# Loading and splitting x and the first two weight slabs in small pieces, in the order of the k tiles

## The reference, cut to what matters

```python
def _rmsnorm(x, g):
    xf = x.astype(jnp.float32)
    y = xf * lax.rsqrt(jnp.mean(xf * xf, axis=-1, keepdims=True) + EPS)
    return (y * g.astype(jnp.float32)).astype(x.dtype)
...
    for l in range(DEPTH):
        h = _rmsnorm(x, g_mix[l])
        p = h @ w_in[l]
```

## Time and profile before

| | |
|---|---|
| runs | 1286.05, 1285.48, 1284.99 us, median 1285.48 |
| profiled execution | span 1283.8 us from the first to the last instruction; no other time of its own is given |
| mean granted TensorE clock | 0.958 |
| busy, share of the span | PE 92%, DVE 58%, ACT 38%, POOL 36% |
| DMA | 108.65 MB, mean 85 GB/s |

### The profile page before, as it was taken

One profiled execution on the slowest core, in us unless ns is written; L12 is line 12 of the kernel. 1 busy time (PEld: TensorE's weight loads), 2 busy tenths in 40 slices (PEclk: granted clock), 3 DMA queues, 4 the chain that ended last, 5 costly groups with the idle time before them and its releaser, 6 DMA issues.

```text
span 1283.8 us, 16689 instructions
## 1 busy us (share of the span) xinstructions
PE 1184.6 (92%) x5302; PEld 963.6 (75%) x5302; DVE 740.4 (58%) x812; ACT 490.1 (38%) x649; POOL 462.8 (36%) x199
## 2 busy tenths in 40 slices
PE   7999999998699979998899999999979999699967
PEld 6788878777588757886778888777757887588856
DVE  5335476677616773377633356757772377716764
ACT  5644244443314432233456323344332343313341
POOL 3423124333443334433533322333333433353341
PEclk8999999999799989998899999999989999899979
DMA  6222113222222222222422211222223222232211
GB/s 256 83 82 72 45 50 99 81 68 81 93 94 75 82 82 89 91 82 82 139 95 68 83 66 36 83 79 69 81 80 99 89 75 82 82 98 84 81 66 66
DMA packets 31681, 108.65 MB, mean 85 GB/s; under 512 B 3722, under 2 KB 3850, under 8 KB 31628
## 3 DMA queue, kind: packets, MB, share of 16 engines
q1 hardware_dynamic: 30396, 105.85, 24.8%
q10 hardware_dynamic: 1232, 2.12, 0.5%
HBM read 105.85 MB, written 2.10 MB: 84 GB/s over the span
## 4 chain that ended last, share of the span: by engine, by line
PE 46%; DVE 36%; ACT 8%; issue 6%; DVEq 2%; ACTq 1%; DMA 1%
DVE arena L830 25%; PE acc L877 10%; PE acc L879 10%; PE acc L878 10%; ACT arena L503 6%; DVE arena L823 5%; PE acc L993 2%; PE acc L994 2%; PE acc L995 2%; DVE arena L835 1%; PE side L1044 1%; DVE xg_lo L554 1%; ACT feat_hi L514 1%; PE side L1064 1%; DVE ssq L561 1%
## 5 line engine op out<-in xcount | busy, mean ns | idle before, releaser
L267 POOL TENSOR_TENSOR w_lo<-w_raw,w_hi 128x1024 fp32r<-128x1024 f32 x192 | 462.2, 2411 | 793.8 <-ACT w_hi L276 793.8
L830 DVE SCALAR_TENSOR_TENSOR arena<-arena,conv_sb 128x512 f32<-128x512 f32 x176 | 322.7, 1833 | 112.3 <-ACT arena L503 99.5
L877 PE MATMUL acc<-xg_hi,w_hi 128*128 128x512 f32 x864 | 345.0, 399 | 15.0 <-POOL w_lo L267 13.7
L879 PE MATMUL acc<-xg_hi,w_lo 128*128 128x512 f32 x864 | 339.1, 392 | 0.0
L878 PE MATMUL acc<-xg_lo,w_hi 128*128 128x512 f32 x864 | 338.9, 392 | 0.0
L276 ACT ACTIVATE w_hi<-w_raw 128x1024 fp32r<-128x1024 f32 x192 | 201.4, 1053 | 251.9 <-PE acc L879 207.1
L877 PE MATMUL acc<-feat_hi,w_hi 128*128 128x512 f32 x480 | 199.8, 416 | 66.4 <-POOL w_lo L267 42.8
L877 PEld LDWEIGHTS acc<-xg_hi,w_hi 128*128 128x128 f32 x864 | 163.5, 189 | 57.6 <-issue 20.9
L878 PE MATMUL acc<-feat_lo,w_hi 128*128 128x512 f32 x480 | 197.0, 410 | 0.0
L879 PE MATMUL acc<-feat_hi,w_lo 128*128 128x512 f32 x480 | 196.1, 408 | 0.0
L879 PEld LDWEIGHTS acc<-xg_hi,w_lo 128*128 128x128 f32 x864 | 163.4, 189 | 34.5
(11 more groups left out here) (133 smaller groups left out, 940.0 us busy)
## 6 DMA issues: line engine op xcount, KB each, us to landing
w_raw<-slabs SPq DMA_DIRECT2D x192, 512.0 KB, 3.3
x<-xT ACTq DMA_DIRECT2D x4, 512.0 KB, 9.6
outT<-arena SPq DMA_DIRECT2D x8, 256.0 KB, 2.1
ln_sb<-ln_gb SPq DMA_DIRECT2D x2, 512.0 KB
spatial_sb<-spatial_w SPq DMA_DIRECT2D x2, 256.0 KB
spatial_b_sb<-spatial_b SPq DMA_DIRECT2D x2, 256.0 KB
gate_sb<-gate_w SPq DMA_DIRECT2D x2, 130.0 KB
rank_raw<-rank_w SPq DMA_DIRECT2D x1, 256.0 KB, 10.5
```

Source lines behind the costliest of these rows:

```text
L267: pool.tensor_tensor(w_lo[:, w], w_raw[:, w], w_hi[:, w].bitcast(F32), ALU.subtract).then_inc(lo_done, 1)
L830: dve.scalar_tensor_tensor(out=z[j], in0=y[j][:, tap:tap + S], scalar=conv_sb[:, bass.ds(coef + tap, 1)], in1=z[j], op0=ALU.mult, op1=ALU. ...
L877: pe.matmul(out, wh, ah, start=first, stop=False)
L879: return pe.matmul(out, wl, ah, start=False, stop=last)
```

## The change

x is loaded in six groups of tiles (0), (1), (2), (3), (4, 5), (6, 7), in turn by ACT's queue (groups 0, 2, 4) and by SP's (1, 3, 5). Slabs 0 and 1 are loaded in three parts each, the columns of k tiles 0 and 1 (128 KB), 2 and 3 (128 KB), 4 to 7 (256 KB), split by ACT and by POOL in the same parts. Semaphores for the parts are added. SP issues rank_raw and slabs 2 and 3 behind these; the other loads keep their order. In the second layer loading and splitting is by whole slabs, as before, but TensorE's order of products is the new one in both layers, with conditions on L for the waits. On DVE gain_lo of 4 and 5 stands ahead of the first two add_square, and add_square of 2 to 5 ahead of rank_lo. ACT's squares are placed between its gains and splits.

The diff, cut to its core:

```diff
--- before.py
+++ after.py
@@ -55,6 +55,9 @@
...
+
+X_GROUPS = ((0,), (1,), (2,), (3,), (4, 5), (6, 7))
+W_PARTS = (slice(0, 2 * P), slice(2 * P, 4 * P), slice(4 * P, SLAB))
 
 def encoder(nc, xT, slabs, rank_w, gate_w, spatial_w, spatial_b, ln_gb, gains, gla_gain, conv, consts, outT):
@@ -164,7 +167,10 @@
             return slot(12 + m)
 
-        x_loaded = [sem(f"x_loaded{i}") for i in range(4)]
+        x_loaded = [sem(f"x_loaded{i}") for i in range(len(X_GROUPS))]
+        raw_part = [[sem(f"raw_part{j}_{part}") for part in range(2)] for j in range(2)]
+        hi_part = [sem(f"hi_part{j}") for j in range(2)]
+        lo_part = [sem(f"lo_part{j}") for j in range(2)]
         gains_loaded, par_loaded = sem("gains_loaded"), sem("par_loaded")
         rank_loaded, vec_loaded = sem("rank_loaded"), sem("vec_loaded")
         raw_loaded = [sem(f"raw_loaded{i}") for i in range(RING)]
@@ -216,6 +222,12 @@
 
             eng.sem_inc(waits_passed, 1)
 
+        def load_x(eng, g):
+            first, n = X_GROUPS[g][0], len(X_GROUPS[g])
+            rows = xT[first * P:(first + n) * P, :].rearrange("(k p) s -> p k s", p=P)
+            eng.dma_start(x[:, first * S:(first + n) * S].rearrange("p (k s) -> p k s", k=n),
+                          rows).then_inc(x_loaded[g], 16)
+
         block = ctx.enter_context(nc.Block())
 
@@ -228,11 +240,29 @@
                              slabs[bass.ds(L * NS + q * RING + j, 1), :, :].rearrange("o p n -> (o p) n")
                              ).then_inc(raw_loaded[j], 16)
 
+            def load_part(j, part):
+                w = W_PARTS[part]
+                sp.dma_start(w_raw[:, j * SLAB + w.start:j * SLAB + w.stop],
+                             slabs[j:j + 1, :, w].rearrange("o p n -> (o p) n")
+                             ).then_inc(raw_part[j][part] if part < 2 else raw_loaded[j], 16)
+
+            load_part(0, 0)
+            load_part(1, 0)
+            load_x(sp, 1)
+            load_part(0, 1)
+            load_part(1, 1)
+            load_x(sp, 3)
+            load_part(0, 2)
+            load_part(1, 2)
+            load_x(sp, 5)
+            sp.dma_start(rank_raw[:, 0:DEPTH * RW], rank_w).then_inc(rank_loaded, 16)
+            load_slab(0, 0, 2)
+            load_slab(0, 0, 3)
             with sp.Fori(0, DEPTH) as L:
-                for j in range(RING):
-                    load_slab(L, 0, j)
+                with sp.If(L > 0):
+                    for j in range(RING):
+                        load_slab(L, 0, j)
                 with sp.If(L < 1):
-                    sp.dma_start(rank_raw[:, 0:DEPTH * RW], rank_w).then_inc(rank_loaded, 16)
                     sp.dma_start(consts_sb[:, :], consts).then_inc(vec_loaded, 16)
                     sp.dma_start(gla_sb[:, :], gla_gain).then_inc(vec_loaded, 16)
                     sp.dma_start(conv_sb[:, :], conv).then_inc(vec_loaded, 16)
@@ -260,7 +290,20 @@
             pool.memset(ones, 1.0).then_inc(ones_set, 1)
             pool.memset(rank_split[:, 2 * RW:2 * RW + P - 4 * RANK].bitcast(F32), 0.0).then_inc(setup_done, 1)
             pool.memset(eps[:, :], EPS).then_inc(lo_done, RING)
-            with pool.Fori(0, DEPTH * NS // RING) as q:
+            for j, part in ((0, 0), (1, 0), (0, 1), (1, 1), (0, 2), (1, 2)):
+                w = slice(j * SLAB + W_PARTS[part].start, j * SLAB + W_PARTS[part].stop)
+                if part < 2:
+                    pool.wait_ge(hi_part[j], part + 1)
+                else:
+                    pool.wait_ge(hi_done, j + 1)
+                pool.tensor_tensor(w_lo[:, w], w_raw[:, w], w_hi[:, w].bitcast(F32),
+                                   ALU.subtract).then_inc(lo_part[j] if part < 2 else lo_done, 1)
+            for j in (2, 3):
+                w = slice(j * SLAB, (j + 1) * SLAB)
+                pool.wait_ge(hi_done, j + 1)
+                pool.tensor_tensor(w_lo[:, w], w_raw[:, w], w_hi[:, w].bitcast(F32),
+                                   ALU.subtract).then_inc(lo_done, 1)
+            with pool.Fori(1, DEPTH * NS // RING) as q:
                 for j in range(RING):
                     w = slice(j * SLAB, (j + 1) * SLAB)
                     pool.wait_ge(hi_done, q * RING + (j + 1))
@@ -307,10 +350,8 @@
                 act.activation(r_ap, side(name)[:, 0:n], ACT.Sqrt, bias=eps[:, 0:1], scale=scale).then_inc(done, 1)
 
             act.dma_start(gains_sb[:, :], gains).then_inc(gains_loaded, 16)
-            for c in range(4):
-                rows = xT[c * 2 * P:(c + 1) * 2 * P, :].rearrange("(k p) s -> p k s", p=P)
-                act.dma_start(x[:, c * 2 * S:(c + 1) * 2 * S].rearrange("p (k s) -> p k s", k=2),
-                              rows).then_inc(x_loaded[c], 16)
+            for group in (0, 2, 4):
+                load_x(act, group)
 
             act.wait_ge(ones_set, 1)
             act.activation(std[:, 0:1], ones[:, 0:1], ACT.Copy)
@@ -320,24 +361,46 @@
 
             act.wait_ge(gains_loaded, 16)
 
-            def load_and_split(c):
-
-                act.wait_ge(x_loaded[c], 16)
-                gain_hi(2 * c, 0)
-                gain_hi(2 * c + 1, 0)
-                act.wait_ge(raw_loaded[c], 16)
-                split_hi(c)
-
-            load_and_split(0)
-            load_and_split(1)
+            def first_gain(group):
+
+                act.wait_ge(x_loaded[group], 16)
+                for m in X_GROUPS[group]:
+                    gain_hi(m, 0)
+
+            def split_part(j, part):
+
+                w = slice(j * SLAB + W_PARTS[part].start, j * SLAB + W_PARTS[part].stop)
+                if part < 2:
+                    act.wait_ge(raw_part[j][part], 16)
+                else:
+                    act.wait_ge(raw_loaded[j], 16)
+                act.activation(w_hi[:, w], w_raw[:, w],
+                               ACT.Copy).then_inc(hi_part[j] if part < 2 else hi_done, 1)
+
+            first_gain(0)
+            split_part(0, 0)
+            split_part(1, 0)
+            first_gain(1)
+            first_gain(2)
+            split_part(0, 1)
+            split_part(1, 1)
+            first_gain(3)
             square(0, 0, 0)
             square(1, 0, 1)
-            load_and_split(2)
-            load_and_split(3)
-            act.wait_ge(rank_loaded, 16)
-            rank_hi(0)
-            for m in range(2, KT):
-                square(m, 0, m)
+            first_gain(4)
+            split_part(0, 2)
+            split_part(1, 2)
+            square(2, 0, 2)
+            square(3, 0, 3)
+            first_gain(5)
+            for j in (2, 3):
+                act.wait_ge(raw_loaded[j], 16)
+                split_hi(j)
+                square(2 * j, 0, 2 * j)
+                square(2 * j + 1, 0, 2 * j + 1)
+                if j == 2:
+                    act.wait_ge(rank_loaded, 16)
+                    rank_hi(0)
 
             with act.Fori(0, DEPTH) as L:
                 def acc_at(n):
@@ -583,14 +646,16 @@
             dve.sem_inc(x_done, RING)
             dve.wait_ge(gains_loaded, 16)
 
-            for m in range(0, 4):
+            for m in range(0, 6):
                 gain_lo(m, 0)
             add_square(0, 0, 0)
             add_square(1, 0, 1)
-            for m in range(4, KT):
-                gain_lo(m, 0)
+            gain_lo(6, 0)
+            gain_lo(7, 0)
+            for m in range(2, 6):
+                add_square(m, 0, m)
             rank_lo(0)
-            for m in range(2, KT):
+            for m in range(6, KT):
                 add_square(m, 0, m)
             dve.wait_ge(vec_loaded, 3 * 16)
             with dve.Fori(0, DEPTH) as L:
@@ -935,28 +1000,38 @@
                     pe.wait_ge(lo_done, L * NS + (n + 1 + RING))
 
-                for tiles in ((0, 1, 2, 3), (4, 5), (6,), (7,)):
-                    for j in range(2):
-                        if tiles[0] == 0:
-                            pe.wait_ge(hi_done, L * NS + (j + 1))
-                            pe.wait_ge(x_done, L * NX + (j + 1))
-                        for k in tiles:
+                for tiles in ((0, 1), (2, 3), (4, 5), (6,), (7,)):
+                    part = min(tiles[0] // 2, 2)
+                    for k in tiles:
+                        for j in range(2):
+                            if k == 0:
+                                pe.wait_ge(x_done, L * NX + (j + 1))
+                            if k == 0:
+                                pe.wait_ge(hi_part[j], 1)
+                                with pe.If(L > 0):
+                                    pe.wait_ge(hi_done, L * NS + (j + 1))
+                            if k == 2:
+                                pe.wait_ge(hi_part[j], 2)
+                            if k == 4:
+                                pe.wait_ge(hi_done, L * NS + (j + 1))
                             if j == 0:
                                 pe.wait_ge(xg_ready, L * 16 + (k + 1))
                             w = w_block(j, k * P)[0]
```

(10 more changed lines are left out.)

## The result

The changed kernel took 1289.77 us, median of 5 runs (1289.30 to 1292.46), against 1285.48 for the kernel before (5 runs, 1284.36 to 1286.05): ratio 1.0041, 95% interval 1.0029 to 1.0054. It is **slower by 4.3 us**. The profiled execution took 1289.30 with a span of 1287.5 (1283.8 before, so 3.7 more). A median over 5 to 23 runs and one traced execution are two things: 23 runs of the kernel before lay between 1282.13 and 1286.90.

What follows compares the result with a forecast made beforehand. The start bounds it: loads, ACT in order, and VectorE with POOL as one resource, up to the spread of ssq at 32.90 us. Terms +2.9 and 0 on 1285.5 gave 1288.4 us, range 1281.4 to 1290.0.

Steps and rivals of the forecast that it cites:

- the mark: Start of the spread of ssq, at 32.90 us before; claimed to move the end by the same amount; forecast +2.9 us.
- Layer 1 and the rest: Second layer, conditions on TensorE's sequencer and work after the mark: claimed to cost 0.
- The turn-taking of VectorE and POOL: In the start, both engines hold one port pair exclusively, so they count as one resource with 21 us of work.
- The loads: In the start, x and slabs 0 and 1 (3.1 MB) come first, at 390 GB/s; x tile 0 at 4.8.
- Rival 4: In the start, x and slab pieces land late, mark at 38.8: +5.9 us, 1291.4; chance 0.08.
- the likeliest case: In the start, splits of slabs 4 and 5 delay rank_lo to 29.6: +2.9 us, 1288.4; chance 0.46.
- rivals 1 and 2: Start: slabs 4 and 5 split after rank_lo, 1284.1 or 1281.5, chance 0.24; only one split before it, 1285.9, chance 0.14.
- the lower third of the forecast's spread: Part of +1.3 to +4.1 us at the mark not above 2.6 us, counted as same with 0.15.
- 0.3 us at 16.1: In the start, margin deciding whether POOL takes slab 2's split ahead of xg_lo 6.
- 1.6 us at 25: In the start, margin between slab 4's high part at 23.4 and addition 5 ending undisturbed near 25.

Runs made afterwards that it cites:

- the second session: The changed kernel run once more as it is, beside the kernel before: 1292.93 us (5 runs) against 1285.16, ratio 1.0065.
- late POOL: Changed kernel, rank_lo behind gain_lo 7, ACT's squares ahead of its splits, POOL's splits of slabs 2 and 3 after all additions: 1278.98 us; again 1278.63.

## Why the prediction was right and wrong

**The step that failed** is the one from the mark to the time: "what moves it moves the end by the same amount", and "Layer 1 and the rest", which the sum has as 0, without a row for the conditions and the rest of the new program. The runs showed +2.46 at the mark, +3.03 at the last outputs, +3.7 in the span and +4.3 between the medians; in the second session +3.5, +5.1, +5.8 and +7.8. Of what the term put at nothing, 0.6 us are the two longer pauses and 0.7 lie behind the start of the last outputs, in every trace of a kernel built on the change; the rest was not settled. The mechanism of the start was right. The second step that failed is the weighing, below: by it the likeliest outcome was no measurable change, and the kernel was measurably slower.

**The start, right nearly line by line.** Forecast against trace: xg_lo 7 ends at 19.8 (20.4), products at 21.1 (22.1), ACT's table load right behind (22.05), slab 4's high part at 23.4 (24.4), POOL's split of slab 4 at 24.1 (24.48; the forecast had it held off by addition 4, in the trace it starts right behind its high part), rank_lo at 29.6 (30.0), pause 8.5 (7.93), rank products 6.2 (5.27, and 6.13 in the second trace), spread +2.9 (+2.46 and +3.5). That the sum is so close is in part luck: rank_lo came 0.4 us later than forecast and the rank products took 0.9 less. The turn-taking of VectorE and POOL, which carries all of it, was shown by taking POOL's splits away: two xg_lo in 1.40 us instead of 3.54, and by holding two of them: rank_lo in 0.42 us instead of 2.5.

**Sums that don't come out.** The range is said to end at the forecast's upper bound, but 1285.5 + 4.1 is 1289.6, not 1290.0; the median 1289.77 lies inside the range as it was given and above the bound as it was worked out. By the terms listed, VectorE and POOL would be busy to 17.4, not 16.9, before slab 2's split, and ACT's gains and splits end at 14.9, not 15.4. Each slip is half a microsecond.

**The loads** came 0.4 to 0.8 us later than I had them: tile 0's gain at 5.27, not 4.9, tile 3's at 9.73. From 4 to 10 us the DMA moved 353 GB/s, where I had taken 390, and 383 from 10 to 17. Rival 4 (pieces land late, +5.9) asked for 3 us, which did not happen: pieces of 128 to 512 KB moved at these rates, and gain 7 started at 15.3 instead of 14.7.

**The size.** The forecast of 1288.4 was 1.4 us short of the median. The second session's median, 1292.93, is 4.5 above it and outside the range of 1281.4 to 1290.0.

**And the chances.** I gave 0.41 to no measurable change and 0.39 to slower, although the likeliest case alone was at +2.9. The "same" was made of rivals 1 and 2 and of the lower third of the forecast's spread. The rivals depended on margins (0.3 us at 16.1, 1.6 us at 25), and these held in all six traces of the changed kernel and its variants without a late POOL: xg_lo 6 always got in before slab 2's split. The first margin was as small as forecast, 16.89 against 17.07 in the changed kernel, but it was 0.17 to 0.18 us in all six, while the start of the split moved from 17.07 to 17.39: loads that came later moved both sides of it. Adding a spread of loads and clock that moves every event together does not make such a race more open, and I had counted it as if it did. The lower third was cut off at 2.6 us, the least that I thought could be told from no change; the measured interval is 1.0029 to 1.0054, some 1.6 us to either side, so most of the forecast's spread would have counted as slower.

**Another term that I took at zero and that was not**: VectorE's order. I costed only rank_lo's displacement. The other half of that edit, gain_lo 4 and 5 ahead of the first additions, makes the order as a whole worth 2.7 us at the spread, without any small piece, although rank_lo's place costs some of it.

## What to carry to other kernels

Where two engines take turns, as VectorE and POOL do here, draw them as one queue: making a third engine faster moves work into that queue, and it may land in front of what the third engine waits for next. Read an early mark and a later one: a wait that is removed at the first can stand in front of the second, with a slow clock behind it. And before loads are cut into pieces, ask which work of the start isn't needed in the start; one wait on POOL in the old kernel gained 4.2 us, the pieces with their order as first written lost 4.3. And an effect of 3 us in 1285 needs more than one trace and one session: the changed kernel lost 4.3 in one and 7.8 in the other.

## What the runs showed of the hardware

- A pause of TensorE costs more than itself: 7.93 us of waiting made the 16 products behind it take 5.27 and 6.13 us in two executions, 3.92 when small products filled the wait, 3.62 with no pause.
- The same pause (7.93 and 7.96 us) is followed by a different number of slow products from one execution to the next: five and nine, besides the first.
- Two executions of one kernel with an equal start end 4.2 us apart (1272.11 and 1267.86 at the last outputs); 2.6 of that come in the first products of the second layer, behind pauses of 2.88 and 1.24 us.
- A quarter of a split alone takes POOL 0.73 us, where a quarter of 2.37 is 0.59. In the changed kernel the six pieces, partly beside VectorE, take 7.1 us (4.05 and 3.09) against 4.77 for the two whole ones before.
